# Moving the mLSTM convolution and SiLU into the input projection, and reordering the mLSTM preparation

## The reference, cut to what matters

```python
mod = c @ w_mod                                        # shift, scale, gate of both halves
h = rmsnorm(x, p['norm1_g']) * (1 + scale1) + shift1
xa, ub, o_pre, ga, gb = jnp.split(h @ p['w_in'], IN_SPLITS, axis=-1)
...
uc = jax.nn.silu(depthwise_conv(u, p['mlstm_conv'], rows))      # 3x3, one row for the context
q = jnp.einsum('bthd,hde->bhte', uch, p['mlstm_w_q'])
k = jnp.einsum('bthd,hde->bhte', uch, p['mlstm_w_k']) * (B_HEAD_DIM ** -0.5)
v = jnp.einsum('bthd,hde->bhte', u, p['mlstm_w_v'])
log_i = uc @ w_i + b_i
log_f = jax.nn.log_sigmoid(uc @ w_f + b_f)
...                                                    # chunked scan over q, k, v, log_i, log_f
```

## Time and profile before

| | us |
|---|---|
| median of 3 runs | 2634.09 (2632.74 to 2639.38) |
| the profiled execution | 2633.48 |
| its span | 2631.8 |
| PE busy | 2163.7 (82%) |
| DVE busy | 1012.3 (38%) |
| ACT busy | 646.9 (25%) |
| POOL busy | 313.1 (12%) |
| mean granted TensorE clock | 0.885 of full speed |

### The profile page before, as it was taken

One profiled execution on the slowest core, in us unless ns is written; L12 is line 12 of the kernel. 1 busy time (PEld: TensorE's weight loads), 2 busy tenths in 40 slices (PEclk: granted clock), 3 DMA queues, 4 the chain that ended last, 5 costly groups with the idle time before them and its releaser, 6 DMA issues. The chain is left out here.

```text
span 2631.8 us, 55427 instructions
## 1 busy us (share of the span) xinstructions
PE 2163.7 (82%) x24137; PEld 1734.2 (66%) x24137; DVE 1012.3 (38%) x2056; ACT 646.9 (25%) x1474; POOL 313.1 (12%) x358
## 2 busy tenths in 40 slices
PE   8899999576757779789699599799999279999950
PEld 8788888536646569579489398245455268788840
DVE  1642232545776354554544544432233200100036
ACT  2301111135634323423323333110011011111111
POOL 0000000006400111111110110311100310000012
PEclk9999999778878679789699699789999589999985
DMA  5232322103222100000000000033221089999955
GB/s 225 86 123 77 147 114 89 51 1 138 74 84 74 74 3 4 32 3 4 31 4 4 31 4 6 16 108 112 91 74 56 17 328 356 358 356 356 352 190 175
DMA packets 65085, 291.34 MB, mean 111 GB/s; under 512 B 7480, under 2 KB 19824, under 8 KB 52336
## 3 DMA queue, kind: packets, MB, share of 16 engines
q1 hardware_dynamic: 47184, 211.20, 22.1%
q0 software_dynamic: 11504, 42.00, 4.6%
q10 hardware_dynamic: 6192, 35.13, 3.5%
HBM read 236.94 MB, written 51.36 MB: 110 GB/s over the span
## 5 line engine op out<-in xcount | busy, mean ns | idle before, releaser
L2353 PEld LDWEIGHTS f_pab<-f_xt,f_w 128*128 128x128 f32 x2240 | 258.1, 194 | 17.4 <-issue 17.4
L2353 PE MATMUL f_pab<-f_xt,f_w 128*128 128x128 f32 x2240 | 258.4, 277 | 0.8 <-ACT f_xt L2383 0.8
L298 PE MATMUL b_ps<-b_h_hi,b_w_lo 128*128 128x512 f32 (+1 forms) x672 | 239.9, 357 | 8.3 <-DVE b_h_lo L347 8.3
L298 PE MATMUL b_ps<-b_h_lo,b_w_hi 128*128 128x512 f32 (+1 forms) x672 | 239.1, 356 | 0.0
L298 PE MATMUL b_ps<-b_h_hi,b_w_hi 128*128 128x512 f32 (+1 forms) x672 | 238.7, 355 | 0.0
L298 PEld LDWEIGHTS b_ps<-b_h_hi,b_w_lo 128*128 128x128 f32 x672 | 128.3, 191 | 26.0 <-issue 8.5
L1704 DVE TENSOR_TENSOR q_zz<-d_two_i,q_pn 128x128 f32<-128x128 f32 x400 | 99.9, 283 | 108.7 <-PE q_pn L1572 108.0
L298 PEld LDWEIGHTS b_ps<-b_h_hi,b_w_hi 128*128 128x128 f32 x672 | 128.1, 191 | 17.6
L298 PEld LDWEIGHTS b_ps<-b_h_lo,b_w_hi 128*128 128x128 f32 x672 | 128.3, 191 | 17.2
L1945 PE MATMUL e_pp<-y,e_wp 128*128 128x512 f32 (+1 forms) x384 | 137.7, 521 | 0.0
L2368 PE MATMUL f_po<-f_w,f_act 128*128 128x512 f32 x280 | 129.0, 603 | 3.8 <-issue 1.0
(11 more groups left out here) (367 smaller groups left out, 4334.9 us busy)
## 6 DMA issues: line engine op xcount, KB each, us to landing
f_w<-in_w SPq DMA_DIRECT2D x35, 2048.0 KB, 8.9
f_w<-in_w SPq DMA_DIRECT2D x35, 1024.0 KB, 9.2
ys_scratch<-f_out ACTq DMA_DIRECT2D x35, 512.0 KB, 8.7
y<-in_w_mod ACTq DMA_DIRECT2D x8, 2048.0 KB, 8.8
w_first<-in_w_in SPq DMA_DIRECT2D x14, 1024.0 KB, 4.8
sig_scratch<-b_stage POOLq DMA_DIRECT2D x20, 640.0 KB, 3.2
c_bc<-row_scratch SPq DMA_DIRECT2D x20, 512.0 KB, 3.8
a_wmod<-in_w_mod SPq DMA_DIRECT2D x4, 2048.0 KB, 19.9
```

Source lines behind the costliest of these rows:

```text
L298: mm = pe.matmul(ps[j % 2][:, n, 0:width], rounded(wt[:, j // 2, k, (j % 2) * P:(j % 2 + 1) * P]), rounded(ht[:, k, first:first + width]), ...
L2353: mm = pe.matmul(pab[:, b, w, f * P:(f + 1) * P], w13[:, b, w, k, f * P:(f + 1) * P], xt[:, b, k], start=(k == 0), stop=(k == KD - 1))
```

## The change

- The 8 modulation parts become 16 of 256 columns, in a tile of their own (`b_wmod`), since the unused half of `c.y` is now taken by the convolution. `b_partial` shrinks to 256 columns per stream and stays a single buffer. `sum_part` is called twice at each of its places.
- DVE's loop is written out; in each of its four rounds it makes one part, convolves one group of 128 channels (11 instructions, each waiting for the one before), makes a second part, then splits two weight pieces.
- ACT's loop is written out; it takes the SiLU in the last round.
- SP loads `w_qkv` and `w_if` into `w_first` after the last split.
- In the preparation, both gates are one product with 128 weight columns (input gate in rows 0 to 35, forget gate in rows 64 to 99), done first; then k of all heads, q of all heads, k by token, v by token. The two exponentials on ACT come after 16 of the 20 copies by token.
- Two tiles of the scan move into `w_first`.

```diff
         h_lo = ctx.enter_context(nc.sbuf_tensor("b_h_lo", [P, KD, NT], F32))
-        wmod = c.y[:, 4:8].rearrange("p a t -> p (a t)")[:, 0:KD * 512].rearrange("p (k n) -> p k n", k=KD)
+        wmod = ctx.enter_context(nc.sbuf_tensor("b_wmod", [P, KD, 256], F32))
+        uc = c.y[:, 4:8]
-        partial = ctx.enter_context(nc.sbuf_tensor("b_partial", [P, 2, 512], F32))
+        partial = ctx.enter_context(nc.sbuf_tensor("b_partial", [P, 2, 256], F32))
...
+            sp.wait_ge(w_split, 14)
+            sp.dma_start(c.w_qkv, io["w_qkv"].rearrange("p a h n -> p (a h n)")).then_inc(next_in, 16)
+            sp.dma_start(c.w_if, io["w_if"].rearrange("p h n -> p (h n)")).then_inc(next_in, 16)
+            sp.wait_ge(next_in, 32)
...
             def sum_part(n):
                 pe.wait_ge(mod_term, n * TERMS + TERMS)
-                for j in range(4):
+                for j in range(2):
...
                 if f in (3, 5, 7):
-                    sum_part((f - 3) // 2)
+                    sum_part(f - 3)
+                    sum_part(f - 2)
...
-                sum_part(i + 3)
+                sum_part(i * 2 + 6)
+                sum_part(i * 2 + 7)
...
+            def convolve(own, k):
...
                 if f % 2 == 1 and f < 7:
                     split_w(1 + f // 4, f % 4 // 2)
-                    make_part((f - 1) // 2)
+                    make_part(f - 1)
+                    make_part(f)
             split_w(2, 1)
-            with dve.Fori(0, 4) as i:
-                make_part(i + 3)
+            dve.wait_ge(copied, 8)
+            own = Own(dve, conv_done)
+            for i in range(4):
+                make_part(2 * i + 6)
+                convolve(own, i)
+                make_part(2 * i + 7)
                 for g in range(2):
                     split_w(i + 3, g)
-            make_part(7)
-            dve.wait_ge(mod_summed, MOD_PARTS - MOD_FIRST)
+            make_part(14)
+            make_part(15)
+            dve.wait_ge(mod_summed, MOD_REST)
...
             for n in range(1, 4):
                 high_w(1 + (n - 1) // 2, (n - 1) % 2)
-                load_part(n)
+                load_part(2 * n - 1)
+                load_part(2 * n)
...
-            with act.Fori(1, 4) as i:
-                load_part(i + 3)
+            for i in range(5):
+                if i:
+                    load_part(2 * i + 6)
                 for j in range(4):
                     sigmoids(i, j)
-                    if j % 2 == 1:
+                    if j == 0:
+                        load_part(2 * i + 7)
+                    if j % 2 == 1 and i < 4:
                         high_w(i + 3, j // 2)
+                    if i == 4 and j == 1:
+                        act.wait_ge(conv_done, CONV_STEPS)
+                        for k in range(BH):
+                            act.activation(uc[:, k], uc[:, k], ACT.Silu).then_inc(uc_set, 1)
...
+            wide(0, [wif[:, k] for k in range(BH)], [uc[:, k] for k in range(BH)], gates_ready)
+            for h in range(BH):
+                if h == 1:
+                    pe.wait_ge(gates_read, 2)
+                elif h >= 2:
+                    pe.wait_ge(wide_dve, h - 1)
+                wide(1 - h % 2, [w[:, 1, h]], [uc[:, h]], wide_ready)
+            for h in range(BH):
+                if h < 2:
+                    pe.wait_ge(wide_dve, 3 + h)
+                else:
+                    pe.wait_ge(wide_act, h - 1)
+                wide(1 - h % 2, [w[:, 0, h]], [uc[:, h]], wide_ready)
             for n in range(NCH):
+                tok(n, uc, 1)
+            for n in range(NCH, 2 * NCH):
                 tok(n, c.y, 2)
...
+            for n in range(NCH):
+                act.wait_ge(tok_ready, n + 1)
+                act.activation(c.ktok[:, n], pt[:, n % 2], ACT.Copy, scale=P ** -0.5).then_inc(tok_read, 1)
             for n in range(NCH, 2 * NCH):
+                if n == NCH + 6:
+                    act.wait_ge(gate_dve, GATE_STEPS)
+                    act.activation(c.rows[:, 1], c.rows[:, 1], ACT.Exp).then_inc(inter_set, 1)
+                    act.activation(c.rows[:, 2], c.rows[:, 3], ACT.Exp, scale=-1.0).then_inc(inter_set, 1)
                 act.wait_ge(tok_ready, n + 1)
+                act.activation(c.vtok[:, n - NCH, :, 0:P], pt[:, n % 2], ACT.Copy).then_inc(tok_read, 1)
```

More of the change, by code:

```diff
@@ L115 @@
 MOD_PARTS, MOD_FIRST = 12, 4
+MOD_REST = 2 * (MOD_PARTS - MOD_FIRST)
 def phase_a(c):
@@ L379, in load_part @@
             def load_part(n):
-                if isinstance(n, int) and n == 0:
+                if n == 0:
                     act.wait_ge(h_split, 3)
@@ L474, in phase_c_prepare @@
         uc = c.y[:, 4:8]
-        w = sb("c_w", [P, 3, BH, P])
-        wif = sb("c_wif", [P, BH, 2, ROWS])
+        w = c.w_qkv.rearrange("p (a h n) -> p a h n", a=3, h=BH)
+        wif = c.w_if.rearrange("p (h n) -> p h n", h=BH)
         bif = sb("c_bif", [ROWS, 2])
@@ L494, in _ @@
         def _(sp):
-            sp.dma_start(w[:, :, :, :], io["w_qkv"]).then_inc(loaded, 16)
-            sp.dma_start(wif[:, :, :, :], io["w_if"]).then_inc(loaded, 16)
             sp.dma_start(bif[:, :], io["b_if"]).then_inc(loaded, 16)
@@ L535, in _, with wide @@
         def _(pe):
-            def wide(n, lhs, rhs, rows):
-                if n >= 2:
-                    pe.wait_ge(wide_act if n % 2 == 0 else wide_dve, (n - 2) // 2 + 1)
+            def wide(bank, lhs, rhs, done):
                 for m, (first, width) in enumerate(BLOCKS):
                     for k in range(len(lhs)):
-                        mm = pe.matmul(ps[n % 2][0:rows, m, 0:width], lhs[k], rhs[k][:, first:first + width],
+                        mm = pe.matmul(ps[bank][:, m, 0:width], lhs[k], rhs[k][:, first:first + width],
                                        start=(k == 0), stop=(k == len(lhs) - 1))
-                mm.then_inc(wide_ready, 1)
+                mm.then_inc(done, 1)
             def tok(n, src, which):
@@ L598, in _ @@
-            assert own.n == CONV_STEPS, own.n
             own = Own(dve, gate_dve)
             own.did(dve.memset(c.rows[:, 3], 0.0))
-            dve.wait_ge(wide_ready, 2)
-            dve.wait_ge(loaded, 96)
+            dve.wait_ge(gates_ready, 1)
+            dve.wait_ge(loaded, 64)
             for m, (first, width) in enumerate(BLOCKS):
-                cp = dve.tensor_scalar(lf[:, first:first + width], ps[1][0:ROWS, m, 0:width], bif[:, 1:2], None, ALU.add)
-                cp.then_inc(wide_dve if m == 2 else gate_dve, 1)
+                cp = dve.tensor_scalar(lf[:, first:first + width], ps[0][64:64 + ROWS, m, 0:width], bif[:, 1:2], None, ALU.add)
+                cp.then_inc(gates_read if m == 2 else gate_dve, 1)
@@ L658, in _ @@
         def _(act):
[L659 to L666 removed]
+            act.wait_ge(loaded, 64)
+            act.wait_ge(gates_ready, 1)
             for m, (first, width) in enumerate(BLOCKS):
                 cp = act.activation(li[:, first:first + width], ps[0][0:ROWS, m, 0:width], ACT.Identity, bias=bif[:, 0:1])
[L669 to L675 removed]
+                cp.then_inc(gates_read if m == 2 else part_read, 1)
+            act.wait_ge(gates_read, 2)
             act.wait_ge(gate_dve, 3)
@@ L711, in phase_c_scan @@
         sem = semaphores(nc, ctx)
-        amask, expo, sd, qi, kw = (sb(f"s_{n}", [P, 2, BH, P]) for n in ("amask", "expo", "sd", "qi", "kw"))
+        amask, expo = (c.w_first[:, 4 * i:4 * i + 4].rearrange("p k n -> p (k n)").rearrange("p (b h t) -> p b h t", b=2, h=BH) for i in range(2))
+        sd, qi, kw = (sb(f"s_{n}", [P, 2, BH, P]) for n in ("sd", "qi", "kw"))
         decay = sb("s_decay", [P, 4, BH])
@@ L2510, in program @@
         c = allocate(nc, ctx, io)
-        with (nc.sbuf_tensor("cs", [P, KD, 2], F32) as c.cs, nc.sbuf_tensor("w_first", [P, KD, 256], F32) as c.w_first,
-              nc.psum_tensor("pm", [P, 4 * MOD_PARTS, 2], F32) as c.pm):
-            phase_a(c)
-            phase_b(c)
-        phase_c(c)
+        with nc.sbuf_tensor("w_first", [P, KD, 256], F32) as c.w_first:
+            flat = c.w_first[:, :, :].rearrange("p k n -> p (k n)")
+            c.w_qkv, c.w_if = flat[:, 0:3 * BH * P], flat[:, 3 * BH * P:4 * BH * P]
+            with (nc.sbuf_tensor("cs", [P, KD, 2], F32) as c.cs,
+                  nc.psum_tensor("pm", [P, 4 * MOD_PARTS, 2], F32) as c.pm):
+                phase_a(c)
+                phase_b(c)
+            phase_c(c)
         phase_d(c)
```

102 lines of the change are left out of this document (37 added, 65 removed).

## The result

| | before | after |
|---|---|---|
| median of 4 runs, us | 2633.41 (2632.13 to 2639.38) | 2653.70 (2653.43 to 2655.35) |
| ratio to the kernel before | 1 | 1.0074, interval 1.0056 to 1.0091 |
| profiled execution, its span | 2633.48, 2631.8 | 2653.55, 2651.8 |
| first store or load of the preparation | 492.83 | 571.57 |
| start of the scan | 615.39 | 629.73 |

The kernel became slower by 20.3 us. Of all runs on record one, of the kernel before beside experiments 1 to 4, was in a slow state (3407.41 us at a clock of 0.631) and is left out of the ratios. By stages of the two profiled executions: phase B and what lies ahead of it +78.7, the preparation -64.4 (122.56 to 58.16), the scan +7.4 (106.57 to 113.96), the rest -1.7. The stage ahead of phase B was 0.45 us shorter after, so the projection itself cost 79.2.

The account below looks back on a forecast made before the run. With TensorE bounding the projection and a serial chain the preparation, the forecast was 2633.48 - 64.0 (preparation) + 77.5 (projection: 34.0 rounds, 23.4 first three places, 15.4 clock, 4.7 end) = 2647.0, 2647.6 as median; range 2631 to 2659.

Parts of the forecast that it names:

- The bound and the handshake: In the projection TensorE sets the pace; with one `b_partial` it waits for DVE's second part 8 times, about 7 us each.
- the handshakes cost nothing: Rival, chance 0.05: both parts of a pair are ready before TensorE needs them, only the saving stands, 2573 us.
- The part: DVE's second half part of 256 columns, 16 instructions that TensorE waits for in the projection: 6.9 us.
- the rival of shorter instructions: Within a rival of chance 0.20: a part in the projection takes 5.5 us, 11.2 us less in all, 2636.4 us.
- The meetings: Projection's added cost of sum, part, split or copy: 8.5 us each in rounds 0 to 3, 7.8 after projections 3, 5, 7.
- The clock: After seven projection stops TensorE restarts at 1.2 GHz, 24 products taking 5.3 instead of 2.9 us: 2.2 each, 15.4 us.
- cheaper handshakes: Rival, chance 0.20: in the projection the clock stays high or returns sooner, 15.4 us less, 2632.2 us.
- The end of phase B: From the sum's start to the next phase 12.9 us instead of 8.2: cost 4.7 us, between 0 and 5.9.
- The convolution at nothing: In the projection's rounds, a convolution group of about 13 us on DVE hides in its wait for TensorE: no cost.
- The preparation: Six steps from its first instruction to the scan: 58.6 us instead of 122.6, 64.0 us saved.
- The rival with the clock falling in the short products: Rival, chance 0.13: preparation's products by token take 1.7 instead of 0.92 us a step, 11 us more, 2658.5 us.
- The step that failed: The scan and what follows, from 615.4 on, was taken as not edited in its work, at no cost.

Follow-up runs that it names:

- experiment 1: Kernel after, with the first sum of each pair moved one projection or two earlier: 2574.85 us, 0.9773 of the kernel before.
- experiment 2: Kernel after, with two buffers for `b_partial` and both sums still at the same place: 2575.18 us, 0.9775 of the kernel before.
- experiment 3: Kernel after, with 30 unused products of 512 columns on TensorE between the two sums of each pair: 2640.12 us, 1.0018 of the kernel before.
- experiment 4: Kernel after, with the scan's two small DVE copies of the normalizer's column written as multiply-add: 2645.80 us, 1.0044 of the kernel before.
- experiment 8: experiment 1 plus the scan's two copies as multiply-add, exponentials after 11 instead of 16 copies by token, transposes after 16 instead of 20: 2566.57 us, 0.9759.
- experiment 5: Kernel before, with the scan's two small DVE copies of the normalizer's column written as multiply-add: 2630.68 us, 1.0004 of the kernel before.
- experiment 6: Kernel after, with `amask` and `expo` in tiles of their own again and `sd` and `kw` in `w_first`: 2645.95 us, 1.0065 of the kernel before.

## Why the prediction was right

The forecast of 2647.6 us had the direction, and 2653.7 lies within its range, 6.1 us above. Point by point:

- **The bound and the handshake**: shown. The observations named in the prediction came: 8 waits of 7 us, 58.1 together; the round at 68.2 us (from 314.36 to 382.54 between two first sigmoids of a round), forecast 67.7. Experiments 1 and 2 take the handshake away in two ways and both come within 2.2 us of the 2573 that the rival "the handshakes cost nothing" gave. As a forecast that rival fell; its price was nearly right, in part by luck: it too left out the scan's loss (7.5 in experiment 1), which a preparation shorter by 65.0 instead of 64, a rest shorter by 2.3 and a projection longer by 0.8 instead of about 3 made up for in most part.
- **The part**: 288.46 to 295.5 is 7.0 us; taken 6.9. A 256-column instruction takes 0.48 us on average on the page of the profile:

```profile
L351 DVE SCALAR_TENSOR_TENSOR b_partial<-b_wmod,cs,b_partial 128x256 f32<-128x256 f32 x224 | 98.7, 482 | 4.0
```

So the rival of shorter instructions (5.5 us a part) falls. The prediction's estimate of 327 ns from the table of the Trainium skill, page "VectorE: DVE Perf Modes", section on the TRN2 errata, is too low as well: the measurement decides, at 482. The advice of that section against small tiles is borne out: two instructions of 256 columns take 0.96 us, one of 512 took some 0.75.
- **The meetings**: at projection 3, from the first sum to the restart, 140.81 to 150.69 is 9.9 us, my steps give 9.65. The second sum ran at 1.2 GHz there, 1.86, which the step left out; it hid for the most part beside DVE's copy.
- **The clock**: it fell at all the restarts looked at, and 24 products took 5.3 us, as taken from the earlier trace rows. In the rounds the rest of 68.2 - 56.9 - 8.5 is 2.8 us each, more than my 2.2; experiment 3 gives 2.5. The rival "cheaper handshakes" falls: it needed a price under 1.4.
- **The end of phase B**: from the first sum (560.18) to the next phase 11.4 us, my steps say 12.9. The meeting after the last two short DVE instructions took 0.8 us, not the 2.7 that I carried over; POOL's store was not the bound. Cost 3.2, not 4.7. The four rounds cost 45.2 (42.8 forecast with their clock), so that 30.8 of the 79.2 are left for the first three places (30.0 forecast). The sum of 77.5 is as near as it is because the end, forecast too dear, made up for part of what the rounds were forecast too cheap.
- **The convolution at nothing**: right. A group runs from 242.39 to 254.1 (11.7 us, 13 estimated) inside DVE's wait for TensorE; in experiment 1 it hides with no loss. A half load took 6.0 us (median of 16 on the page of the profile), not 4.8, within the 9 allowed; DVE waited 8.7 us for them in all, TensorE for none.
- **The preparation**: 58.2 against 58.6, every one of the six steps within 0.4 us (gates 11.3 for 11.4, gate chain 21.5 for 21.8 and 39.7 for 40.0, exponentials 45.5 for 45.8). The rival with the clock falling in the short products fell: up to the exponentials the steps kept 0.92 us. It was near, though: behind the exponentials TensorE had stood for 3.06 us, and the last copies came 1.7 us apart (621.45 to 623.16), here at no cost. In experiment 8 the same stop stood earlier and took away what the early exponentials gave.
- **The step that failed**: "What comes after 615.4 is not edited in its work." True of the work, but the change moved two tiles of the scan into the weights' buffer. The scan was costed at nothing and cost 7.4, more than all that the forecast was short of. The profiled execution is 6.55 above the sum of 2647.0: scan 7.4, projection +1.7, preparation -0.4, the stage ahead of phase B -0.45, what follows the scan -1.7. Experiments 4 and 5 put it on two copies of four columns and what they hold up, experiment 6 ties their length to the moved tiles; why the copies wait that long stays open.

## What to carry to other kernels

When a step is cut in two and both halves are consumed at the same place, look at the buffer between them: with one buffer, producer and consumer take turns, and a producer that was free became a full wait, 8 times here. A second buffer, or one of the two sums moved ahead by one or two projections, turned +20 us into -58. Where the engine that stops is TensorE, add to the stop itself what the restart at 1.2 GHz costs, here 2.4 to 2.8 us each; and where DVE copies beside GpSimd, look at the duration of the smallest copies in the profile, not only at the large ones.

## What the runs showed of the hardware

- A DVE copy of four elements per partition lasted 2.55 to 7.72 us beside GpSimd's work, each one looked at ending within 0.1 us of a boundary between two instructions of GpSimd; as a multiply-add of the same operands it took 0.84 to 0.86 us.
- Filling TensorE's stop with products did not keep the clock in every round: a wait of 1.13 us behind them was in some rounds followed by the 1.2 GHz level, in others not.
- After a stop of 3.06 us in the products by token (experiment 8) the 1.2 GHz level came too; the earlier trace rows had shown it after 4.3 us.
- A load of 1 MB took 6.0 us for the half parts of `w_mod`, which lie in runs of 1 KB, and 4.7 us for the pieces of `w_first` (medians of the issues on the page of the profile after). They also differ in their queue and in what runs beside them, so that the runs' length is the cause isn't shown:

```profile
b_wmod<-in_w_mod ACTq DMA_DIRECT2D x16, 1024.0 KB, 6.0
...
w_first<-in_w_in SPq DMA_DIRECT2D x14, 1024.0 KB, 4.7
```
